# Mixer projection with one 512-column moving operand, and VectorE emptying the projection banks

## The reference

```python
h = rms_norm(x, norm_mix_w[l])
proj = h @ w_in[l]                     # 256 x 2048 by 2048 x 6160
q, k, v, z, b, a, rx, rgate = jnp.split(proj, split_points, axis=-1)
y_gdn = gated_deltanet_group(q, k, v, z, b, a, ...)   # 8 heads of 128, chunks of 64 tokens
y_rg = rglru_group(rx, rgate, ...)                    # 8 blocks of 128
x = x + jnp.concatenate([y_gdn, y_rg], axis=-1) @ w_out[l]
x = x + hierarchical_moe(rms_norm(x, norm_ffn_w[l]), ...)   # 32 experts, top 2
return rms_norm(x, norm_final_w)
```

## Time and profile before

| what | value |
|---|---|
| runs of the kernel before | 1729.54, 1732.15, 1735.81 us, median 1732.15 |
| profiled execution, first to last instruction (span) | 1727.7 us |
| PE busy, matmuls | 1534.4 us, 89%, 8398 |
| DVE busy, instructions | 665.6 us, 39%, 1144 |
| ACT busy, instructions | 393.2 us, 23%, 735 |
| POOL busy, instructions | 211.8 us, 12%, 152 |
| mean granted clock of TensorE | 0.967 of full speed |

### The profile page before, as it was taken

The page is one execution under the profiler, slowest core; times in us unless marked ns, Lnnn a source line. Parts: engine busy times, 40 slices in busy tenths (PEclk is TensorE's granted clock), DMA queues, the critical chain, the costliest instruction groups (busy, mean ns, idle before and its releaser), DMA issues.

```text
span 1727.7 us, 21935 instructions
## 1 busy us (share of the span) xinstructions
PE 1534.4 (89%) x8398; PEld 939.2 (54%) x8398; DVE 665.6 (39%) x1144; ACT 393.2 (23%) x735; POOL 211.8 (12%) x152
## 2 busy tenths in 40 slices
PE   5888988988986986889999999989989999999996
PEld 4787878888885765443443444344344344344342
DVE  6866677667666354102202212212221221221223
ACT  5435435434434243000111011011011001001002
POOL 2233224224223243000000000000000000000000
PEclk9999999999998998899999999999999999999999
DMA  7543334334342348499999999999999999999994
GB/s 213 130 101 97 101 100 100 97 100 100 97 154 100 98 155 307 154 402 396 395 403 395 397 401 395 399 399 395 402 396 395 403 395 398 400 395 400 398 395 175
DMA packets 268459, 480.88 MB, mean 278 GB/s; under 512 B 11081, under 2 KB 111634, under 8 KB 251026
## 3 DMA queue, kind: packets, MB, share of 16 engines
q1 hardware_dynamic: 268434, 480.54, 77.3%
HBM read 478.43 MB, written 2.10 MB: 278 GB/s over the span
## 4 chain that ended last, share of the span: by engine, by line
PE 61%; DVE 16%; DMA 9%; ACT 6%; issue 5%; SPq 2%; DVEq 0%; ACTq 0%
PE bank L519 60%; DMA ew<-in_expert_w_dram 9%; DVE w_parts L1151 2%; SPq L488 2%; PE bank L522 2%; ACT w_parts L881 1%; DVE ew L1190 1%; DVE misc L1283 1%; DVE misc L1282 1%; ACT ew L1077 1%; DVE ye L1252 1%; DVE ye L1183 1%; DVE ye L1190 1%; DVE ew L1527 1%; ACT hT L1072 1%
## 5 line engine op out<-in xcount | busy, mean ns | idle before, releaser
L519 PE MATMUL bank<-ew,hT 128*64 128x512 f32 (+1 forms) x1600 | 461.4, 581 | 18.5 <-ACT hT L1072 14.0
L519 PE MATMUL bank<-act_parts,w_parts 128*128 128x256 f32 x2304 | 333.8, 298 | 22.2 <-DVE w_parts L1151 17.4
L519 PEld LDWEIGHTS bank<-ew,hT 128*64 128x64 f32 (+1 forms) x1600 | 158.9, 137 | 294.4 <-issue 290.5
L519 PEld LDWEIGHTS bank<-act_parts,w_parts 128*128 128x128 f32 x2304 | 299.1, 198 | 35.3 <-DVE w_parts L1151 19.2
L519 PE MATMUL bank<-ew 128*64 128x512 f32 (+1 forms) x1056 | 240.8, 600 | 21.9 <-DVE ew L1529 19.8
L519 PE MATMUL bank<-mixT,hT 128*64 128x512 f32 x512 | 225.8, 594 | 0.0
L1527 DVE SCALAR_TENSOR_TENSOR ew<-ew,bank 128x256 f32<-128x256 f32 x32 | 13.5, 421 | 515.3 <-ACT ew L1079 515.3
L1594 POOL TENSOR_TENSOR w_parts<-fw,w_parts 128x768 fp32r<-128x768 f32 x64 | 136.6, 2142 | 337.5 <-ACT w_parts L881 337.3
L519 PEld LDWEIGHTS bank<-ew 128*64 128x64 f32 (+1 forms) x1056 | 84.6, 140 | 163.8 <-issue 158.1
L519 PE MATMUL bank<-ye,ew 128*128 128x512 f32 x256 | 122.8, 612 | 15.2 <-DVE fw L1515 13.7
L881 ACT ACTIVATE w_parts<-fw 128x1024 fp32r<-128x1024 f32 x128 | 128.4, 1051 | 16.7 <-PE bank L519 16.4
(11 more groups left out here) (221 smaller groups left out, 1078.2 us busy)
## 6 DMA issues: line engine op xcount, KB each, us to landing
ew<-in_expert_w_dram SPq DMA_DIRECT2D x160, 2048.0 KB, 18.1
mixT<-in_expert_w_dram SPq DMA_DIRECT2D x32, 2048.0 KB, 19.2
fw<-in_w_in_dram SPq DMA_DIRECT2D x48, 1024.0 KB, 5.9
fw<-in_w_out_dram SPq DMA_DIRECT2D x16, 1024.0 KB, 5.1
mixT<-in_x_dram SPq DMA_DIRECT2D x1, 2048.0 KB, 7.6
fw<-in_x_dram SPq DMA_DIRECT2D x1, 2048.0 KB, 10.0
out_dram<-fw SPq DMA_DIRECT2D x2, 1024.0 KB, 3.9
ye<-in_norm_ffn_w_dram SPq DMA_DIRECT2D x1, 1024.0 KB, 4.7
```

The costliest lines, as they stand in the source:

```text
L519: return nc.tensor.matmul(o, l, r, start=start, stop=stop, skip_group_check=True)
```

## The change

For every chunk of a block PE now issues two matmuls in place of three. The first has the high weights and, as one moving operand, the high and the low activations of the chunk, 2 x 256 columns; it writes all 512 columns of the bank, high by high into the first half and high by low into the second. The second has the low weights and the high activations and adds to the first half. The two halves of the bank have to be added when it is emptied: DVE does so with a `tensor_reduce` over pairs, 48 in all, and ACT's copies go. ACT's tanh for z reads `zr` in SBUF, waits for DVE's count and reports on a new semaphore `s_thz`, for which `silu_z` waits.

```diff
                 for b in range(6):
                     o = bank[b % 2][:, 0:T]
+                    both = bank[b % 2][:, :].rearrange("p (a t) -> p a t", a=2)
...
                     for k in range(KD):
-                        mm(o, w[:, 0, k, :], parts[:, 0, k, :], k == 0, False)
-                        mm(o, w[:, 0, k, :], parts[:, 1, k, :], False, False)
+                        mm(both, w[:, 0, k, :], parts[:, :, k, :], k == 0, k == KD - 1)
                         l = mm(o, w[:, 1, k, :], parts[:, 0, k, :], False, k == KD - 1)
...
             def evac(h, b, halves=(0, 1)):          # on ACT
-                act.wait_ge(s_proj, h * 6 + b + 1)
-                src = bank[b % 2][:, 0:T]
                 if b == 3:
-                    act.activation(thz, src, ACT.Tanh, scale=0.5)
-                act.activation((th[:, 0], th[:, 1], th[:, 2], zr, xr, gg)[b], src, ACT.Copy).then_inc(s_evac, 1)
+                    act.wait_ge(s_evac, h * 6 + 4)
+                    act.activation(thz, zr, ACT.Tanh, scale=0.5).then_inc(s_thz, 1)
...
+            def evac(h, b):                         # on DVE
+                dve.wait_ge(s_proj, h * 6 + b + 1)
+                V.tensor_reduce((th[:, 0], th[:, 1], th[:, 2], zr, xr, gg)[b],
+                                bank[b % 2][:, :].rearrange("p (a t) -> p t a", a=2), AX.X, ALU.add).then_inc(s_evac, 1)
...
             def silu_z(h):
+                dve.wait_ge(s_thz, h + 1)
                 V.scalar_tensor_tensor(sz, thz, 1.0, zr, ALU.add, ALU.mult)
...                                                  # head 0, ahead of the loop
             for b in range(3):
+                if b == 2:
+                    evac(0, 2)
                 conv(0, b)
                 if b:
                     rest(b + 3, b)
+                if b == 2:
+                    evac(0, 3)
                 silu(0, b)
...                                                  # in the loop
                     if n == 0:
                         params(i)
+                        evac(i, 0)
                         conv(i, 0)
                     elif n == 1:
                         silu(i, 0)
+                        evac(i, 1)
                         conv(i, 1)
...
                     elif n == 3:
+                        evac(i, 2)
                         conv(i, 2)
+                        evac(i, 3)
...
                 heads(i - 1, pre, between)
+                evac(i, 4)
                 rest(i * 6 + 6, 0)
                 conv_rx(i)
+                evac(i, 5)
                 silu_z(i)
```

More of the change, by code:

```diff
@@ L319, in build @@
         s_evac = sem("s_evac")
+        s_thz = sem("s_thz")
         s_rx = sem("s_rx")
@@ L1166, in _ @@
             dve.wait_ge(s_bath, 2)
+            evac(0, 0)
             log1p(B[6], B[3], B[5], B[7], B[0])
             rest(3, 0)
+            evac(0, 1)
             link(V.tensor_tensor(B[5], B[4], B[6], ALU.add))
@@ L1324, in _ @@
             rest(6, 0)
+            evac(0, 4)
             conv_rx(0)
             rest(7, 1)
+            evac(0, 5)
             silu_z(0)
```

## The result

The changed kernel takes 1758.47 us (median of 4 runs, 1755.05 to 1759.76), the kernel before beside it 1731.53: a ratio of 1.015, with a 95% interval of 1.0134 to 1.0167. The forecast was 1753.8, between 1743 and 1776. Both profiled executions have a mean granted clock of 0.967; their spans are 1753.3 and 1727.7 us.

What follows compares the result with a forecast made beforehand. PE was taken to wait twice a turn for DVE's chain with the convolution of q, and again at the turn-over. 1727.7 + 6.0 (start) + 16.1 (seven turns of 2.3) - 0.5 = span 1749.3, plus 4.45: 1753.8 us, range 1743 to 1776.

Steps and rivals of the forecast that it cites:

- The matmuls, 0.2 us a turn: PE's chunks: two matmuls for three save 0.010 us per chunk, with some 20 chunks a turn on the path.
- The price of one reduction, 0.69: DVE's reduction from a bank costs 0.69 us, by the elements read, between 0.48 and 0.96.
- `evac(i, 0)`, 0.4: Levels, block 0's reduction ahead of the convolution of q, in the chain PE waits for: 0.4 us, between 0 and 0.7.
- `evac(i, 1)`, nothing: Block 1's reduction between levels 2 and 3, where DVE idles 0.68 us: costs nothing, though without a margin.
- Block 4, 1.15: Chunks of a turn: PE stands about 1.15 us until block 2's bank is emptied behind the copy of S; 0.9 to 1.4.
- The turn-over, 0.95: Reductions of blocks 4 and 5 ahead of `select`: 0.25 and 0.69 us, counted as 0.95, between 0.7 and 1.4.
- The start, 6.0: Head 0: reductions in DVE's gapless chain, coupled with ACT's queue, make the end 6.0 us later, give or take 2.
- Sum: Start 6.0 plus seven turns 16.1, less 0.5 in the first: 21.6 us more, span 1749.3, time 1753.8.
- The clock (1): Rival, chance 0.22: a new stall or longer turn-over brings another half-clock stretch, up to 1.7 us each turn: 1766, two 1778.
- Nothing covered (2): Rival, chance 0.12: each of the four reductions outside the chunks costs its full 0.69 us; 3.7 a turn, 1764 us.
- PE sets the pace (3): Rival, chance 0.07: DVE has time for every reduction, so only the matmuls' saving of 7.8 us is left: 1724, at most 1698.
- Cover nearly complete (4): Rival, chance 0.07: levels and `evac(i, 4)` cost nothing, block 4's stall is 0.5 us, the start 2: 1738 us.

Runs made afterwards that it cites:

- DVE's order alone: Kernel before, with DVE's work in a turn put in another order and neither half of the change: 1698.36 us, ratio 0.981.
- both orders: The 512-column matmul alone, with ACT still copying: on the kernel before 1734.63 us, on the kernel with DVE's turn reordered 1701.59 us.
- the doubling: Changed kernel, one reduction of the seven turns done twice, first result thrown away: block 0 1761.34 us, block 1 1770.24, block 4 1763.41.
- second profile of the change: The changed kernel timed and profiled again with no edit: 1756.48 us, ratio 1.0148 to the kernel before, span 1753.2.

## Why the prediction was right, step by step

- **What bounds the kernel.** Right, and shown from both sides: DVE's order alone is worth 33 us, fewer matmuls nothing. Part of the 33 is the clock: the loop has four half-clock stretches there, and thirteen in the kernel before.
- **The matmuls, 0.2 us a turn.** The direction was right for PE, and the kernel's time does not show it. A run of 18 chunks takes 6.51 us where it took 6.73, 3% less, as forecast. Turns alike in their clock are 0.10 to 0.12 us shorter on both orders, half of the forecast; on the order of before the time was even 0.15% longer, since more turn-overs ran at half clock. The page's 131 ns for a matmul of 512 columns (Trainium skill, TensorE: Matmul & The Clock Gate, Back-to-back issue gap) is not what this type does (0.233 us). Nor does the Trainium skill say there that the time per chunk would nearly halve, as I wrote: with that section's 81 ns for 128 columns and 131 for 512, a matmul of 256 columns lies between, and a chunk would take 212 to 262 ns for 243 to 393, an estimate, a third less at most.
- **The price of one reduction, 0.69.** Right: 0.684, by the elements read. At 365.24 it ran beside POOL's masks and took no longer. The Trainium skill (SBUF — State Buffer, Who interferes with whom) says that `tensor_reduce` never contends for the shared port; the trace agrees, 680 to 693 ns over all 48.
- **`evac(i, 0)`, 0.4.** The number came out too low for the wait and about right for the turn. PE's resume after the first mask is 5.64 us (365.10 to 370.74), before 4.97: 0.67, the full length. The first chunk of block 2 then follows after 5.96 us, before 6.37: 0.41 is given back there. The reason that I gave, that DVE's tap instructions would slip out of POOL's reach, is wrong: the three taps take 2.56 against 2.58, since the masks cover them still. What was given back lies behind L1283. In the doubling, too, most of it was given back there: 0.3 to 0.4 a turn.
- **`evac(i, 1)`, nothing.** The number came out, the reason did not, and that is luck. DVE's gap of 0.68 ahead of level 3 did not hold the reduction: it took the gap, POOL's low part of block 3 moved in among the taps (3.01 against 1.52), and DVE needs 1.5 us more from the update of level 2 to that of level 3. PE waits 1.3 us there. What hid it is the clock: behind the second wait PE no longer runs at half clock (three chunks at 294.64 took 2.04 us, the same three at 377.87 take 1.28), so level 2's update comes 3.4 us behind the end of that wait (376.70 to 380.09) where it came 5.0 behind (292.65 to 297.61), and from the end of that wait to PE's matmuls of level 3 it is 9.2 us (376.70 to 385.89) for 9.4 (292.65 to 302.00). I had no such term. Why the clock no longer falls there, behind a wait of 1.66 us in place of 1.92, stays open. The levels as a whole, from the broadcast to the last chunk of block 3, cost 0.07 us (43.88 for 43.81), where I had 0.4.
- **Block 4, 1.15.** Right in mechanism, place and size. The row says 0.90 of idle time, 5.8 us in seven; but counted as I counted, from when block 4 wanted to start (396.88 + 0.36 = 397.24) to when it did (398.39), it is 1.15. PE was at the place about when I said: the chunk before block 4 starts 43.88 us behind the broadcast. Moving the reduction took the wait away and 1.1 us a turn with it.
- **The turn-over, 0.95.** 0.68 from og to the broadcast. I expected 0.25 for `evac(i, 4)` and it was 0.08 from og on (`rest` is 0.43 us shorter, and the first reduction follows og 0.1 us sooner than `rest` did); `evac(i, 5)` was 0.60, for 0.69. Doubling showed that the cover was `rest`'s 0.43 us of hold, and that it is used up: L1189 still takes 1.94.
- **The start, 6.0.** 6.6 at the broadcast, and 8.5 by PE's first wait in the levels (9.1 less the 0.67 of the first turn), since PE ran at half clock from 80 to 90 us; the clock had no term in the start. Block 4 began at 63.28 (forecast 63.7), `silu(0, 2)` at 69.77 (70.7); the coupling through ACT is confirmed by taking it away.
- **Sum.** Forecast 2.3 a turn, and 0.5 less in the first. In the turn shown it is 1.82 (66.28 for 64.46): 0.07 in the levels, 1.07 from there to the last chunks of block 5, the matmuls' saving included, and 0.68 in the turn-over. Seven times this is 12.7 us, but the seven turns lose 19.1 (468.72 for 449.62): the other 6.4 lie in turns in which the two kernels' half-clock stretches differ. In the second profile of the change, with other turn-overs at half clock, (543.9 - 77.5) / 7 - 64.5 = 2.1. So my turn was 0.5 too dear and the clock, which I had left out of the sum, made up for it and more: span 1749.3 forecast, 1753.3 and 1753.2 measured, 21.6 us more forecast, 25.6 measured. That the number came so near is in part luck. The 4.45 us from span to median, too, is no cost around the span: each run of the change lies 1.7 to 1.9 us above its own span, and the rest is that the profiled execution of the kernel before was the fastest of its runs.
- **The rivals.** The clock (1): true in part. The mean of the loop is 0.95 as before, but that is a sum of fewer stretches in one place and more in others. None comes behind the new wait at block 4; in three turn-overs and at the start one does, up to three in a row, and a turn with one takes 0.9 us longer, the one with two 2.4. By my own sign ("one more stretch at half clock") the forecast fails in turns 1, 4 and 7. Nothing covered (2): nearly true of `evac(i, 5)`, in DVE's time true of `evac(i, 1)`, half true of `evac(i, 0)`, false of `evac(i, 4)`. PE sets the pace (3): refuted. Cover nearly complete (4): true of the levels and `evac(i, 4)`, refuted at block 4 and in the start.

## What to carry to other kernels

Before you spare an engine that looks full, ask what it waits for at the fixed places of a turn: here fewer matmuls gave nothing while the order of VectorE's work gave 2%. A gap of an engine is no cover for work that also shifts its neighbours: count the gap used up when another engine's instruction can move into what follows. Compare turns and not only means: a mean clock of 0.95 in both kernels hid half-clock stretches that had moved, and the turns in which they differ lost up to 6.4 us more, more than the error of any term. A releaser named `issue`, or one that ended long ago, hides another; look for the last of the parts that the instruction needs.

## What was not expected of the hardware

- A reduction over pairs from a bank (512 elements read, 256 written, float32) takes 0.684 us with hardly any spread, beside POOL too, while `conv_rx`'s first instruction takes 1.94 us in POOL's company and 0.41 alone.
- VectorE's taps are held for as long as POOL's instruction lasts and then run on: three of them took 1.52, 2.56, 3.01 or 3.33 us, by what POOL did beside them.
- With 700 matmuls fewer in the same stretch the granted clock was 0.93 against 0.95 on one order of the work, and 0.98 against 0.98 on the other.
- The same wait can have half clock behind it or not. In the other order every turn has a wait of 2.17 or 2.18 us before block 2; the turns with half clock behind it take 60.6 us, those without 59.04, and with the wait gone the loop ran at a granted clock of 1.00 throughout.
